# Attention of a two-layer block: TensorE starts gate chunks before the projections are finished, and ScalarE's and VectorE's side work stands elsewhere

## The reference, cut to what matters

```python
h = modulate(rms_norm(x, norm1_g[l]), sh1, sc1)
qa, ka, va, qb, kb, vb, ga, gb = split_in_proj(h @ w_in[l])
ya = window_attention_latent(apply_rope(qa), apply_rope(ka), va, kac, vac, sink_a[l])   # 8 heads, band of +-128
yb = full_attention_latent(apply_rope(rms_norm(qb)), apply_rope(rms_norm(kb)), vb, kbc, vbc)  # 8 heads, all keys
x = x + gt1 * (sigmoid(ga) * (ya @ w_pa) + sigmoid(gb) * (yb @ w_pb)) @ w_o
```

## Time and profile before

| | |
|---|---|
| median of 3 runs | 2652.49 us (2652.48 to 2653.84) |
| profiled execution, its own time | 2660.09 us |
| its span | 2658.3 us |
| TensorE, weight loads, VectorE, ScalarE busy | 91%, 76%, 59%, 42% of the span |
| mean granted TensorE clock | 0.958 of full speed |

### The profile page before, as it was taken

One profiled execution on the slowest core, in us unless ns is written; L12 is line 12 of the kernel. 1 busy time (PEld: TensorE's weight loads), 2 busy tenths in 40 slices (PEclk: granted clock), 3 DMA queues, 4 the chain that ended last, 5 costly groups with the idle time before them and its releaser, 6 DMA issues.

```text
span 2658.3 us, 32137 instructions
## 1 busy us (share of the span) xinstructions
PE 2426.4 (91%) x12095; PEld 2008.4 (76%) x12095; DVE 1562.9 (59%) x2383; ACT 1105.5 (42%) x1752; POOL 132.3 (5%) x243
## 2 busy tenths in 40 slices
PE   6978888889799999999797999889999989988898
PEld 2767777778678888888675777678888867867687
DVE  2664657678855555553675677653333367377763
ACT  2435656752332122122444677343222255456451
POOL 0000000011000000000000000100000000000010
PEclk9999989999899999999898999999999989989999
DMA  5211011145343333332221111423222224512153
GB/s 222 104 43 47 35 36 42 42 173 211 111 160 128 118 135 127 118 111 72 96 79 44 48 48 48 170 74 101 96 95 95 94 93 143 170 65 65 67 190 111
DMA packets 67744, 267.68 MB, mean 101 GB/s; under 512 B 8416, under 2 KB 8480, under 8 KB 66448
## 3 DMA queue, kind: packets, MB, share of 16 engines
q1 hardware_dynamic: 41616, 154.16, 16.9%
q0 software_dynamic: 25984, 111.55, 11.7%
HBM read 237.37 MB, written 27.26 MB: 100 GB/s over the span
## 4 chain that ended last, share of the span: by engine, by line
PE 77%; DVE 9%; ACT 7%; issue 6%; DMA 1%; POOL 0%; POOLq 0%; ACTq 0%; DVEq 0%
PE ps L183 21%; PE ps L184 21%; PE ps L185 21%; PE ps L969 1%; PE ps L971 1%; PE ps L970 1%; ACT pr L1024 1%; ACT hf L419 1%; PE ps L953 1%; PE ps L488 1%; DVE wt_out L313 1%; PE ps L910 1%; PE ps L917 1%; DVE maxes L1105 1%; DVE w_lo L179 1%
## 5 line engine op out<-in xcount | busy, mean ns | idle before, releaser
L183 PE MATMUL ps<-h_hi,w_hi 128*128 128x512 f32 (+1 forms) x2328 | 874.0, 375 | 89.9 <-DVE spread L1141 25.6
L184 PE MATMUL ps<-h_lo,w_hi 128*128 128x512 f32 (+1 forms) x2328 | 857.9, 368 | 0.0
L185 PE MATMUL ps<-h_hi,w_lo 128*128 128x512 f32 (+1 forms) x2328 | 856.7, 368 | 0.0
L183 PEld LDWEIGHTS ps<-h_hi,w_hi 128*128 128x128 f32 x2328 | 450.3, 193 | 178.2 <-issue 68.6
L184 PEld LDWEIGHTS ps<-h_lo,w_hi 128*128 128x128 f32 x2328 | 450.6, 194 | 74.0 <-issue 2.1
L185 PEld LDWEIGHTS ps<-h_hi,w_lo 128*128 128x128 f32 x2328 | 448.8, 193 | 76.4
L179 DVE TENSOR_TENSOR w_lo<-w_raw,w_hi 128x1024 fp32r<-128x1024 f32 x288 | 351.4, 1222 | 256.3 <-ACT w_hi L172 255.9
L172 ACT ACTIVATE w_hi<-w_raw 128x1024 fp32r<-128x1024 f32 x288 | 302.9, 1053 | 336.5 <-PE ps L185 312.4
L185 PE MATMUL ps<-q_hi,w_lo 128*128 128x512 f32 x720 | 257.0, 357 | 0.0
L184 PE MATMUL ps<-q_lo,w_hi 128*128 128x512 f32 x720 | 256.7, 357 | 0.0
L183 PE MATMUL ps<-q_hi,w_hi 128*128 128x512 f32 x720 | 256.3, 356 | 0.0
(11 more groups left out here) (331 smaller groups left out, 2933.8 us busy)
## 6 DMA issues: line engine op xcount, KB each, us to landing
w_raw<-in_stream SPq DMA_DIRECT2D x288, 512.0 KB, 3.3
wt<-in_ada_t POOLq DMA_DIRECT2D x80, 512.0 KB, 3.6
ada_raw<-in_ada POOLq DMA_DIRECT2D x4, 2048.0 KB, 15.2
x_keep<-x POOLq DMA_DIRECT2D x8, 768.0 KB, 5.7
gates<-th_g POOLq DMA_DIRECT2D x16, 384.0 KB, 2.6
x<-x_keep POOLq DMA_DIRECT2D x2, 3072.0 KB, 12.8
gates<-sg POOLq DMA_DIRECT2D x24, 256.0 KB, 2.3
gates<-th_g POOLq DMA_DIRECT2D x16, 256.0 KB, 2.3
```

The source lines that it names most:

```text
L183: nc.tensor.matmul(out_ap, lh, rh, start=start, stop=False)
L184: nc.tensor.matmul(out_ap, lh, rl, start=False, stop=False)
L185: return nc.tensor.matmul(out_ap, ll, rh, start=False, stop=stop)
```

## The change: what it does

1. The attention's `phase` now has `follows_on`: no engine waits for the whole stage before it. What each needs from `project` it waits for by name (the dictionary `proj`).
2. Seven gate chunks (`early = PRO + AHEAD` = 14 ahead of step 0, where it was 8) now stand ahead of the wait for `ready`, right behind the last matmul of `project`. The rest is spread over the steps as before.
3. In layer 1 gate units alternate between two places in PSUM (`GB` = 2), so a unit waits for the tanh of the unit two before.
4. `place` and `free_after`: a context tile with an odd number has its scores in the other bank. Latent tiles stay where they were.
5. VectorE takes the maximum of a step's tile ahead of the low part.
6. ScalarE: the second `prep` copy, the `sums` copy and the weight split each move one step later than their partner. `divide` and `split_lo` on VectorE move one step with them.
7. GpSimd clears `qb` as soon as `x` is stored away.

```diff
-            LAG, PRO = 2, 8
+            GB = 1 if both else 2
+            gate_at = lambda u: 512 * (u % GB)
+            LAG, PRO, AHEAD = 2, 8, 6
...
-            upto = lambda t: t + PRO + 1 if t < 0 else min(CHUNKS, PRO + -(-(CHUNKS - PRO) * (t + 1) // (T - 3)))
+            early = PRO + AHEAD
+            upto = lambda t: t + early + 1 if t < 0 else min(CHUNKS, early + -(-(CHUNKS - early) * (t + 1) // (T - 3)))
...
+            def place(m):
+
+                n, qt = tiles[m]
+                a, b = keys(n, qt)
+                w = b - a
+                if m % 2 == 0 or w:
+                    return 1024 + SEQ, 1024 + SEQ - w, 1024 + SEQ - w, 1024 + TOK
+                return 1024, 1024, 1024, 1024 + CTX
+
+            def free_after(m):
+
+                banks = lambda k: set(range(place(k)[2] // SEQ, (place(k)[3] - 1) // SEQ + 1))
+                return max([k + 1 for k in range(m) if banks(k) & banks(m)], default=0)
...
-                        if q:
-                            e.wait_ge(gated.sem, gated.base + q // CH)
+                        if q >= GB * CH:
+                            e.wait_ge(gated.sem, gated.base + q // CH - GB + 1)
...
-                    if m:
-                        e.wait_ge(maxed.sem, maxed.base + m)
+                    if free_after(m):
+                        e.wait_ge(maxed.sem, maxed.base + free_after(m))
...
-                e.wait_ge(ready.sem, ready.base + 4)
+                e.wait_ge(proj["copied"].sem, proj["copied"].base + proj["T"] - 1)
+                e.wait_ge(proj["squared"].sem, proj["squared"].base + proj["n_sq"][proj["T"] - 1])
...
-                    for q in todo[:1]:
+                    now = todo if t == -PRO else todo[:1]
+                    for q in now:
                         gate_chunk(q)
+                    if t == -PRO:
+                        e.wait_ge(ready.sem, ready.base + 4)
...
-                    if u + 2 <= N_GATE:
-                        split_hi(e, base + u + 3)
...
+                        if final[n] + LAG + 2 == t:
+                            y_sums(n)
+                    for u in ends_at(t - 1):
+                        if u + 2 <= N_GATE:
+                            split_hi(e, base + u + 3)
                     for h in range(len(heads)):
                         if prep_at[h] == t:
-                            prep(h)
+                            prep(h, heads[h][2])
+                        if prep_at[h] + 1 == t:
+                            prep(h, 1 - heads[h][2])
...
-                    if 0 <= t < T:
-                        lower(t)
                     for m in range(M):
                         if tile_at[m] == t:
                             tile_max(m)
+                    if 0 <= t < T:
+                        lower(t)
...
-                        since = t - (final[n] + LAG + 2 + 2 * (u % parts))
+                        since = t - (final[n] + LAG + 3 + 2 * (u % parts))
...
-                   (stored[0], 8 * N_GATE), (stored[1], 8 * N_GATE)], pe=pe, act=act, dve=dve, pool=pool)
+                   (stored[0], 8 * N_GATE), (stored[1], 8 * N_GATE)], follows_on=True, pe=pe, act=act, dve=dve, pool=pool)
```

More of the change, by code:

```diff
@@ L813, in project @@
                   + ([(y_kept, 1)] if norm.passes == 2 else []), follows_on=True, pe=pe, act=act, dve=dve, pool=pool)
-            return dict(T=T, copied=copied, shaped=shaped, n_qk=n_qk[T], spilled=spilled, here=here)
+            return dict(T=T, copied=copied, shaped=shaped, n_qk=n_qk[T], spilled=spilled, here=here, squared=squared, n_sq=n_sq, low=low,
+                        n_hl=n_hl[T], v_low=v_low, n_v=n_v[T], q_done={j: n_qk[t + 1] for t, (k, j) in enumerate(kinds) if k == "Q"})
         def layer_tiles(layer, both):
@@ L820, in layer_tiles, with attention_and_gates @@
                     ("v", 1, TOK, None, False, 1.0)] + [("Q", j, w, qg if j >= 4 else None, True, sc) for j in range(8)]
-        def attention_and_gates(layer, both):
+        def attention_and_gates(layer, both, proj):
             nonlocal u0
@@ L945, in tile_scores @@
                         e.wait_ge(a_ready.sem, a_ready.base + 2 * h + 2)
-                    if m:
-                        e.wait_ge(maxed.sem, maxed.base + m)
+                    if m == 0:
+                        e.wait_ge(proj["copied"].sem, proj["copied"].base + proj["T"])
+                        e.wait_ge(proj["squared"].sem, proj["squared"].base + proj["n_sq"][proj["T"]])
+                        e.wait_ge(proj["low"].sem, proj["low"].base + proj["n_hl"])
+                        e.wait_ge(table_done, 3)
+                    if free_after(m):
+                        e.wait_ge(maxed.sem, maxed.base + free_after(m))
                     a, b = keys(n, qt)
+                    ctx_at, lat_at = place(m)[0:2]
                     at = (4 * c + qt) * P
@@ L1002, in pe @@
                         values(t - LAG)
-                    for q in todo[1:]:
+                    for q in todo[len(now):]:
                         gate_chunk(q)
@@ L1009, in act, with prep @@
             def act(e):
-                def prep(h):
+                def prep(h, side):
                     kind, j, g = heads[h]
@@ L1052, in gate @@
                         e.wait_ge(stored[u % 2].sem, stored[u % 2].base + 16 * (u // 2))
-                    nc.scalar.activation(th_g[:, u % 2, 0:wide], psf[:, 0:wide], ACT.Tanh, scale=0.5).then_inc(gated.sem, 1)
-                    if u + 2 <= N_GATE:
-                        split_hi(e, base + u + 3)
+                    if u == 0:
+                        e.wait_ge(proj["shaped"].sem, proj["shaped"].base + proj["n_qk"])
+                        e.wait_ge(proj["low"].sem, proj["low"].base + proj["n_hl"])
+                        e.wait_ge(table_done, 3)
+                    nc.scalar.activation(th_g[:, u % 2, 0:wide], psf[:, gate_at(u):gate_at(u) + wide], ACT.Tanh, scale=0.5).then_inc(gated.sem, 1)
                 def y(n):
@@ L1061, in y, with y_sums @@
                     e.wait_ge(valued.sem, valued.base + final[n] + 1)
+                    nc.scalar.activation(qf[half[g], 4 * kind + j, s0:s0 + w], ps[half[g], 6 + n % 2, 0:w], ACT.Copy).then_inc(y_taken.sem, 1)
+                def y_sums(n):
+                    h, c = items[n]
+                    kind, j, g = heads[h]
+                    s0, w = queries(n)
                     if h >= 2:
                         e.wait_ge(divided.sem, divided.base + (h // 2 - 1) * parts + c + 1)
-                    nc.scalar.activation(qf[half[g], 4 * kind + j, s0:s0 + w], ps[half[g], 6 + n % 2, 0:w], ACT.Copy).then_inc(y_taken.sem, 1)
                     nc.scalar.activation(sums[half[g], s0:s0 + w], ps[half[1 - g], 6 + n % 2, 0:w], ACT.Copy).then_inc(y_taken.sem, 1)
-                for t in range(-PRO, T + LAG + 1):
+                for t in range(-PRO, T + LAG + 2):
                     if 0 <= t < T:
@@ L1152, in dve @@
                         split_lo(e, base + 2)
-                    for u in ends_at(t):
+                    for u in ends_at(t - 1):
                         if u + 2 <= N_GATE:
```

23 lines of the change are left out of this document (15 added, 8 removed).

## The result

The changed kernel takes 2596.6 us (median of 4 runs, 2595.4 to 2598.1) against 2653.2 us of the kernel before in the same comparison; the ratio is 0.978, 95% interval 0.977 to 0.980. That is 56.6 us or 2.1% less, inside the stated range of 2550 to 2615, 17.6 us over the 2579 that I named and just outside the 2568 to 2595 to which I gave the largest chance. The profiled execution took 2595.56 us, with a span of 2593.8 us.

The account below looks back on a forecast made before the run. TensorE's waits in the attention stages, from clumped ScalarE and VectorE work, were the bound. Starts 14, layer 0 waits 29, layer 1 waits 16, clock 13: 72, with tenths 73 us, from 2652.5 to 2579 us; range 2550 to 2615.

Parts of the forecast that it names:

- What bounds it: Both attention stages: TensorE waits because ScalarE's and VectorE's work comes in clumps; neither is the bound as a whole.
- The starts: Start of each attention stage: earlier first scores and six more chunks done gain 14 us, bounds 10 and 18.
- The waits of layer 0: Layer 0's attention, maxima first and ScalarE spread: some 29 of 40.6 us of waits for maxima and tanh go.
- 1.85 us less ahead would leave no wait: Layer 0 heads: with tanh and weight split on other steps, the wait of at most 1.7 us would vanish.
- the 12 us: Layer 0's attention: waits expected to be left, 0.75 us a head for 16 heads.
- The waits of layer 1: Layer 1's attention: of 20.7 us of waits for maxima and tanh 5 stay, so 16 go; bounds 10 and 19.
- The clock: TensorE's clock in both attention stages: 13 us come back as long waits go, bounds 4 and 17.
- the sixth taken off: Both attention stages: about a sixth of the reduced-clock loss falls while TensorE stands still anyway.
- The rival in which short waits keep the clock down: TensorE's clock: pauses of one to two microseconds lower it, the 13 us don't come back; 2592 us, chance 7%.
- ScalarE's clump only changes shape: Attention: TensorE waits for Q's second half in nearly every head; 41 us gained, 2611 us, chance 22%.
- low parts come late: Attention: low parts over 2 us behind lock three engines to their latency; 96 us added, 2676 us, chance 4%.
- a border at 2.5 us: TensorE in the attention stages: its clock falls after waits of 2.5 us and more.

Follow-up runs that it names:

- Experiment 2: Kernel before with only VectorE's order changed, a step's maximum taken ahead of its low part: 2626.0 us, ratio 0.988.
- Experiment 6: Kernel before with only ScalarE's Q copies moved two steps earlier, both halves together, VectorE's order as it was: 2629.2 us, ratio 0.989.
- experiment 3: Changed kernel with ScalarE lumped again (second Q copy, sums and weight split back in their partners' steps): 2596.6 us, ratio 0.977.
- Experiment 8: Changed kernel without the six further early gate chunks, one ahead of the wait for the memsets in place of seven: 2607.4 us, ratio 0.982.
- Experiment 9: Changed kernel with the common wait ahead of the attention put back, the seven early chunks kept: 2610.7 us, ratio 0.983.
- experiment 4: Changed kernel with both Q copies on ScalarE two steps earlier: 2574.6 us, ratio 0.970.

## Why the prediction was right, and where its sum was off

*What bounds it.* Right: clumps on ScalarE, passed on by VectorE's order. Experiments 2 and 6 show both links by themselves, 31 and 27 us. But of the two parts of the change that were to remove it, only VectorE's order did (13.5 us inside the changed kernel); ScalarE's spreading gave 3 us at most (experiment 3).

*The starts, forecast 14 us.* Right. Counted from L629, the first scores came 1.8 us earlier in layer 0 and 1.5 us in layer 1 (1375.08 - 1357.56 = 17.5 against 19.0), and with six chunks of 1.06 and 0.7 us done that is 8.1 + 5.7 = 13.8 us. Experiments 8 and 9 lose 10 to 14. The table load for the tanh was covered, as forecast: it runs at 193.20 and 1370.72, while TensorE stands still. I had overlooked that it was not covered before. There it stood at 208.27 and 1420.37, 1.28 us each, right ahead of a tanh for which TensorE then waited 1.09 us (to 210.52) and 2.51 us (to 1422.40). In layer 0 a wait of 1.0 us for the first tanh is still there; in layer 1 it is gone. The pause in layer 1 that is left is 8.52 us, not the 3 to 4 I named for layer 0 (4.00): chunks of 512 columns are shorter (0.7 us against 1.06), so seven don't fill the time. More early chunks there were not tried.

*The waits of layer 0, forecast 29 us of 40.6.* This is the term that was mis-sized most. Of 41.8 us in all 23.9 are left, so 17.9 went. That the second Q copy would be late was right. What failed is the sentence "1.85 us less ahead would leave no wait", by which I put the wait at 0.75 us a head: waits for Q alone came to 15.7 us in 16 heads, 1.0 a head. The waits are there in heads where ScalarE entered the two steps idle (286.44 above), 1.0 us in five heads and up to 2.5 in others: mainly not the backlog but the two steps' own work, 6.1 us of ScalarE's against 4.7 of TensorE's between its `make` at 285.77 and the point where it is ready at 290.51, makes them. And steps without a chunk, of which there are now 14 in layer 0 (8 before), leave 1 us less cover; the two longest of these waits, 2.08 us (to 292.59) and 2.46 us (to 435.82), end such steps. In a few full heads a weight split still stood ahead of the second copy (411.32 and 433.85). Tanh waits, which I had inside the 12 us, stayed at 6.7 us by themselves.

*The waits of layer 1, forecast 16 us.* Half right: tanh waits went (6.5 to none), maxima fell from 14.2 to 6.1, but 3.9 us of waits for ScalarE's copies are new; in all 23.3 became 12.1, 11 us.

*The clock, forecast 13 us.* Mis-sized the other way. Deficit 17.5 + 3.6 = 21.1 us before, by the same sum 1.7 us now (0.01 x 173.8): with the sixth taken off, 16 us came back. That is an estimate: the clocks of the windows are rounded to 0.01, which is some 3 us over both stages, and no experiment changed the clock alone. The rival in which short waits keep the clock down is refuted for these stages: 147 us with eight waits of 1.0 to 2.1 us ran at 1.00.

13.8 + 17.9 + 11.2 + 16 = 58.9 us against 59.8 of the stage lengths, where I had forecast 72: the account closes within the rounding of the clock term. That does not prove each term, since in experiment 4 the same sum of waits leaves 6.5 us open. That the result fell into the range is in part owed to its width, 65 us: the waits were set 16 us too high and the clock 3 us too low. Of the rivals, "ScalarE's clump only changes shape" (41 us) named the right mechanism, and the result lies between it and the forecast. That low parts come late was not seen: 0.2 us in layer 0 and 1.1 us in layer 1 at its end. The memset on GpSimd moved to 88.30 and 1288.4 us and nothing waits for it.

## What to carry to other kernels

When work is spread to break up a clump, lay out each spread piece against its reader: a piece moved later that an engine waits for costs what the others gain. Move such pieces earlier, into steps where their engine has room; here that was worth 22 us where spreading later was worth 3 us at most. In a queue served in order, put what frees the bound engine ahead of what waits for a third engine; these two lines alone gave 31 us, and 13.5 us beside the rest of the change.

## What the runs showed of the hardware that I had not expected

The length of a wait does not decide by itself whether TensorE's clock falls to the lower of its two levels. In the changed kernel a wait of 1.97 us at 413 us was followed by a reduced clock, one of 2.46 us at 436 us was not:

```profile
413.00:420.00 7.00, 6.70 (x26) 5.55 (x27) 4.91 (x7) 4.10 (x9) 0.00 (x0) 0.76 0.22 75
435.00:442.00 7.00, 6.18 (x31) 5.24 (x32) 4.67 (x6) 5.12 (x9) 0.00 (x0) 1.00 0.21 75
```

Nor does the kernel before bear out a border at 2.5 us, as I had put it in the prediction. There a wait of 2.25 us at 402.02 was followed by a granted clock of 0.61 over the next 4 us, and one of 2.64 us at 262.94 by 1.00.

The Trainium skill ("TensorE: Matmul & The Clock Gate", section "What's actually happening") says that the clock gate's activity window is free-running and doesn't reset when a kernel starts. The two rows above are consistent with that but do not show it, since what TensorE did ahead of the two waits differs too.
